# Pick products moved to GpSimd, ScalarE and TensorE, and the value gates loaded into two buffers of 8 tiles

## The reference

```
h = rms_norm(x);  q = h @ w_pq                        # 8 heads, two halves of 128
sc = q . sub_keys                                     # 2 x 128 scores per head
top 16 of each half -> 256 sums -> top 16 -> expert = i1 * 128 + i2;  gate = softmax(best)
a   = u_emb[expert] . h                               # one dot product per token, head, pick
out = sum over 8 * 16 picks of gelu(a) * gate * v_emb[expert]
```

## Time and profile before

| | us |
|---|---|
| median of three runs | 4348.66 |
| the profiled execution | 4346.32 |
| its span | 4344.6 |
| VectorE busy | 3200.2 (74%) |
| TensorE busy | 3476.6 (80%) |
| GpSimd busy | 1899.8 (44%) |
| ScalarE busy | 1453.4 (33%) |

### The profile page before, as it was taken

How to read it: one execution, slowest core, us unless ns; L and a number is a source line. 1 busy time by engine, 2 the same in 40 slices (tenths; PEclk the granted TensorE clock), 3 DMA queues, 4 the chain that set the end, 5 groups by cost and what they waited for, 6 DMA issues and landing times. The chain is left out here.

```text
span 4344.6 us, 46851 instructions
## 1 busy us (share of the span) xinstructions
PE 3476.6 (80%) x15298; PEld 2697.7 (62%) x15298; DVE 3200.2 (74%) x5528; ACT 1453.4 (33%) x2400; POOL 1899.8 (44%) x1508
## 2 busy tenths in 40 slices
PE   6999999997999987789899999733377777777775
PEld 5776667774778765577777777523355555555554
DVE  5677777777535137999999999899856666666667
ACT  3555555556524332232323232222211111111112
POOL 2443334433221314456565656455434444444443
PEclk9999999998999999899999999855588888888887
DMA  2111111102533225799999999898878888888785
GB/s 89 44 45 50 49 50 49 54 25 89 202 126 122 78 83 196 269 357 358 359 360 356 368 361 366 297 375 325 330 249 285 289 284 289 291 284 289 285 290 213
DMA packets 333363, 964.44 MB, mean 222 GB/s; under 512 B 30912, under 2 KB 96704, under 8 KB 330048
## 3 DMA queue, kind: packets, MB, share of 16 engines
q0 software_dynamic: 147456, 536.94, 33.3%
q1 hardware_dynamic: 183360, 390.95, 25.9%
q10 hardware_dynamic: 2304, 33.56, 1.9%
HBM read 861.18 MB, written 100.14 MB: 221 GB/s over the span
## 5 line engine op out<-in xcount | busy, mean ns | idle before, releaser
L2444 POOL DMA_INDIRECT spread_vrow<-in_v_rows,shared_pick_rows x512 | 712.4, 1391 | 769.7 <-DVE spread_y L2472 654.8
L1582 POOL DMA_INDIRECT ret_urow<-in_u_rows,shared_pick_rows x512 | 641.0, 1252 | 469.4 <-DVE ret_urow L2193 331.0
L157 PE MATMUL spread_banks<-spread_ahi,spread_vhi 128*128 128x512 f32 x1024 | 457.1, 446 | 344.7 <-DVE spread_alo L2484 260.8
L2472 DVE SCALAR_TENSOR_TENSOR spread_y<-spread_vrow,shared_pick_coef,spread_y 128x1024 f32<-128x1024 f32 x512 | 638.8, 1279 | 8.8 <-DMA spread_vrow<-in_v_rows,shared_pick_rows 8.8
L2193 DVE SCALAR_TENSOR_TENSOR ret_urow<-ret_urow,ret_h_rows 128x1024 f32<-128x1024 f32 x512 | 608.9, 1227 | 17.9 <-DMA ret_urow<-in_u_rows,shared_pick_rows 15.6
L157 PE MATMUL shared_carry<-ret_hhi,shared_w_hi 128*128 128x512 f32 x1152 | 474.2, 412 | 106.3 <-DVE shared_w_lo L1382 63.2
L157 PEld LDWEIGHTS spread_banks<-spread_ahi,spread_vhi 128*128 128x128 f32 x1024 | 213.6, 209 | 458.5 <-DVE spread_alo L2484 287.4
L157 PE MATMUL shared_carry<-shared_wide_hi,shared_w_hi 128*128 128x512 f32 x1152 | 458.3, 398 | 27.4 <-DVE shared_wide_lo L585 11.2
L158 PE MATMUL shared_carry<-ret_hlo,shared_w_hi 128*128 128x512 f32 x1152 | 464.9, 404 | 0.0
L159 PE MATMUL shared_carry<-shared_wide_hi,shared_w_lo 128*128 128x512 f32 x1152 | 453.7, 394 | 0.0
L158 PE MATMUL shared_carry<-shared_wide_lo,shared_w_hi 128*128 128x512 f32 x1152 | 453.7, 394 | 0.0
(11 more groups left out here) (295 smaller groups left out, 6921.2 us busy)
## 6 DMA issues: line engine op xcount, KB each, us to landing
spread_vraw<-in_peer_v SPq DMA_DIRECT2D x128, 512.0 KB, 6.9
shared_w_raw<-in_peer_u SPq DMA_DIRECT2D x65, 512.0 KB, 7.0
gelu_u<-shared_front SPq DMA_DIRECT2D x128, 256.0 KB, 8.0
gates<-spread_stage ACTq DMA_DIRECT2D x16, 2048.0 KB, 9.5
spread_act<-gelu_u SPq DMA_DIRECT2D x128, 256.0 KB, 5.3
spread_graw<-gates SPq DMA_DIRECT2D x32, 1024.0 KB, 15.5
ret_wraw<-in_peer_u SPq DMA_DIRECT2D x63, 512.0 KB, 6.8
shared_w_raw<-in_w_mix SPq DMA_DIRECT2D x56, 512.0 KB, 3.4
```

Of the source, the lines that this page charges most:

```text
L157: nc.tensor.matmul(out, whi, xhi, start=(first and i == 0), stop=False)
L1582: nc.gpsimd.indirect_dma_start(slots[s][:], None, u_rows, bass.IndirectOffsetOnAxis(tables.rows[:, t, hd * K + j:hd * K + j + 1], 0)).then ...
L2444: nc.gpsimd.indirect_dma_start(v_slots[s][:], None, v_rows, bass.IndirectOffsetOnAxis(tables.rows[:, t, j:j + 1], 0)).then_inc(row_loaded[ ...
L2472: nc.vector.scalar_tensor_tensor(out=y[:, t], in0=v_slots[s][:], scalar=tables.coef[:, t, j:j + 1], in1=y[:, t], op0=ALU.mult, op1=ALU.add ...
```

## The change

**Dot products.** From dot 34 on (the second block with dots) every fourth, 120 in all, is not done by VectorE. GpSimd multiplies the row in its slot by `h` (`product`), behind the fetches of the two next rows and after waiting for this row to land. ScalarE sums the products with a copy that accumulates (`sums`), behind the tile to whose place in the order the dot belongs (`due`). The slot is free when ScalarE has summed. The slots stay 7.

**Early rows of v.** In the one-hot stage TensorE weighs three of the four rows of each step: ScalarE scales the identity by the coefficients (`diag`, six buffers), TensorE multiplies it with the row (two plain f32 matmuls of 512 columns) and accumulates in four banks of PSUM, for tokens of blocks 0 and 1. VectorE adds these sums to `y` once, after the stage. The slots for rows of `v` go from 13 to 7, in the value groups too.

**Value gates.** `graw` becomes two buffers of 8 tiles (2 MB each, runs of 1 KB), loaded once per two groups. The activations' buffer moves to a place of its own, so that its first tiles are loaded before the last gates are stored.

```diff
@@ -1512,6 +1512,10 @@
+        FIRST_POOLED, POOL_BEHIND = dots_before(2), 2
+        pooled = [d >= FIRST_POOLED and d % 4 == 3 for d in range(DOTS)]
+        upto = {kind: [sum(p is kind for p in pooled[:d]) for d in range(DOTS + 1)] for kind in (True, False)}
...
@@ -1577,8 +1581,10 @@
                     pool.wait_ge(rows_made, hd + 1)
-                pool.wait_ge(dotted, d + 1)
-                pool.sem_inc(slot_held, 1)
+                if d >= ROWS_SLOTS:
+                    last = d - ROWS_SLOTS
+                    pool.wait_ge(pool_summed if pooled[last] else dotted, upto[pooled[last]][last + 1])
+                    pool.sem_inc(slot_held, 1)
...
@@ -1591,10 +1597,20 @@
             pool.wait_ge(x2t_stored, 16 * GT)
+            def product(d):
+                s, t = d % ROWS_SLOTS, d % (GT * K) % GT
+                pool.wait_ge(row_loaded[s], d // ROWS_SLOTS * 16 + 16)
+                nc.gpsimd.tensor_tensor(slots[s][:], slots[s][:], h_rows[:, t], ALU.mult).then_inc(pool_dotted, 1)
...
                 fetch(d)
+                if d >= POOL_BEHIND and pooled[d - POOL_BEHIND]:
+                    product(d - POOL_BEHIND)
...
                     give_low((d - ROWS_SLOTS + 1) // 3 + 3)
+            for d in range(DOTS - POOL_BEHIND, DOTS):
+                if pooled[d]:
+                    product(d)
...
@@ -1927,16 +1943,39 @@
+            summed_to = [0]
...
+            def sums(upto_dot):
...
+                for d in range(summed_to[0], max(upto_dot, summed_to[0])):
+                    if pooled[d]:
+                        hd, k, s = d // (GT * K), d % (GT * K), d % ROWS_SLOTS
+                        t, j = k % GT, k // GT
+                        act.wait_ge(pool_dotted, upto[True][d + 1])
+                        nc.scalar.activation(slots[s][:], slots[s][:], ACT.Copy,
+                                             accum_out=tables.coef[:, t, hd * K + j:hd * K + j + 1]).then_inc(pool_summed, 1)
+                summed_to[0] = max(upto_dot, summed_to[0])
...
+            def due(tile):
...
+                n = tiles.place[tile]
+                b = max(b for b in range(FIRST_DENSE, BLOCKS) if STARTS[b] <= n)
+                first, after = dots_before(b), dots_before(b + 1)
+                return min(after, first + (after - first) * (n - STARTS[b]) // (STARTS[b + 1] - STARTS[b]))
...
                     expert(e)
+                    sums(due(("expert", 1, e)))
...
                             query(b + 1, c)
+                            sums(due(("query", b + 1, c)))
...
                         copy_scores(b + 1)
+            sums(DOTS)
...
@@ -1946,7 +1985,8 @@
                 parts_high(r)
-            act.wait_ge(dotted, DOTS + ROWS_SLOTS)
+            act.wait_ge(dotted, upto[False][DOTS])
+            act.wait_ge(pool_summed, upto[True][DOTS])
...
@@ -2187,6 +2227,8 @@
                 for d in range(d0, d1):
+                    if pooled[d]:
+                        continue
...
@@ -2320,7 +2362,8 @@
         QC = NC // NQ
-        SV = 13
+        SV = 7
+        G8 = 2 * E
...
@@ -2331,8 +2374,8 @@
-        act = m.at("act", [P, E, TD], F32, at(36))
-        graw = m.at("graw", [P, QUARTERS, E, W], F32, at(44))
+        act = m.at("act", [P, E, TD], F32, at(176))
+        graw = [m.at(f"graw{i}", [P, QUARTERS, G8, W], F32, at(x)) for i, x in enumerate((36, 160))]
...
@@ -2342,19 +2385,23 @@
+        DIAGS = 6
+        diag = [m.at(f"diag{i}", [P, P], F32, at(184) + 512 * i) for i in range(4)] + [m.at(f"diag{4 + i}", [P, P], F32, at(189) + 512 * i) for i in range(2)]
...
+        y_sums = banks[:, NB:NB + 4].rearrange("p (t h) n -> p t (h n)", h=2)
...
@@ -2365,12 +2412,27 @@
         FIRST_PICKS = EARLY * N
+        BY_PE = 3
+        order, made_of = [], [0] * GT
+        for d in range(PICKS):
+            if d < FIRST_PICKS:
+                n, i = divmod(d, EARLY)
+                t = (BY_PE * n + i) % 2 if i < BY_PE else 2 + n % 2
+            else:
+                t = min((t for t in range(GT) if t != order[-1][0]), key=lambda t: made_of[t])
+            order.append((t, made_of[t]))
+            made_of[t] += 1
+        by_pe = [d < FIRST_PICKS and d % EARLY < BY_PE for d in range(PICKS)]
+        upto = {kind: [sum(p is kind for p in by_pe[:d]) for d in range(PICKS + 1)] for kind in (True, False)}
+        PE_PICKS = upto[True][PICKS]
+        before = [max([x for x in range(d) if order[x][0] == order[d][0] and by_pe[x] is by_pe[d]], default=None) for d in range(PICKS)]
...
@@ -2384,11 +2446,11 @@
-            def load_gates(g):
-                if g:
-                    sync.wait_ge(weighted, E * g)
-                sync.dma_start(graw[:].rearrange("p n e t -> p n (e t)"),
-                               g_out[:, :, E * g:E * g + E, :].rearrange("n p j t -> p n (j t)")).then_inc(g_loaded, 16)
+            def load_gates(i):
+                if i >= 2:
+                    sync.wait_ge(weighted, G8 * (i - 1))
+                sync.dma_start(graw[i % 2][:].rearrange("p n e t -> p n (e t)"),
+                               g_out[:, :, G8 * i:G8 * i + G8, :].rearrange("n p j t -> p n (j t)")).then_inc(g_loaded[i % 2], 16)
...
@@ -2401,14 +2463,14 @@
                 load_values(1, q)
+            for e in range(E):
+                load_tile(0, e)
...
                 sync.wait_ge(stored[s], 16 * (QUARTERS // SLOTS))
-            for e in range(E):
-                load_tile(0, e)
             load_gates(0)
+            load_gates(1)
...
                 load_tile(1, e)
-            load_gates(1)
...
@@ -2418,7 +2480,8 @@
                 load_tile(g, 3)
-                load_gates(g)
+                if g % 2 and g < NG - 1:
+                    load_gates(g // 2 + 1)
...
@@ -2437,10 +2500,16 @@
             def fetch(d):
-                s, t, j = d % SV, d % GT, d // GT
-                pool.wait_ge(picked, d + GT + 1)
-                pool.sem_inc(slot_held, 1)
+                s, (t, j) = d % SV, order[d]
+                if d >= SV:
+                    last = d - SV
+                    pool.wait_ge(weighed if by_pe[last] else picked, upto[by_pe[last]][last + 1])
+                    pool.sem_inc(slot_held, 1)
...
@@ -2466,18 +2535,24 @@
                 for d in range(d0, d1):
-                    s, t, j = d % SV, d % GT, d // GT
+                    if by_pe[d]:
+                        continue
+                    s, (t, j) = d % SV, order[d]
                     dve.wait_ge(row_loaded[s], d // SV * 16 + 16)
-                    dve.wait_ge(picked, d + SV + 1)
+                    if before[d] is not None:
+                        dve.wait_ge(picked, upto[False][before[d] + 1])
+                    elif t < 2:
+                        dve.wait_ge(y_joined, t + 1)
...
                 dve.wait_ge(a_loaded[e], g * 16 + 16)
-                if e == 0:
-                    dve.wait_ge(g_loaded, g * 16 + 16)
+                gates, i = graw[g // 2 % 2], g % 2 * E + e
+                if i == 0:
+                    dve.wait_ge(g_loaded[g // 2 % 2], g // 4 * 16 + 16)
                 tokens = act[:, e].rearrange("p (n t) -> p n t", t=W)
-                tt(tokens, tokens, graw[:, :, e], ALU.mult).then_inc(weighted, 1)
+                tt(tokens, tokens, gates[:, :, i], ALU.mult).then_inc(weighted, 1)
...
@@ -2508,6 +2583,9 @@
                 split(0, e)
+            dve.wait_ge(weighed, PE_PICKS)
+            for t in range(2):
+                tt(y[:, t], y[:, t], y_sums[:, t], ALU.add).then_inc(y_joined, 1)
...
@@ -2578,10 +2656,21 @@
                     mm.then_inc(g_done, 1)
+                for d in range(EARLY * n, EARLY * n + BY_PE):
+                    s, (t, j) = d % SV, order[d]
+                    last = d + 2 >= FIRST_PICKS - EARLY + BY_PE
+                    pe.wait_ge(row_loaded[s], d // SV * 16 + 16)
+                    pe.wait_ge(diag_made, upto[True][d + 1])
+                    for h in range(2):
+                        mm = nc.tensor.matmul(y_sums[:, t, h * H:h * H + H], diag[upto[True][d] % DIAGS][:], v_slots[s][:, h * H:h * H + H],
+                                              start=(j == 0), stop=last)
+                    mm.then_inc(weighed, 1)
...
                     q, dp = k // QC, slice(k % QC * P, k % QC * P + P)
+                    if g == 0 and k in (4, 6):
+                        pe.wait_ge(y_joined, k // 2 - 1)
...
@@ -2615,6 +2704,13 @@
                     values(0, n)
+                for d in range(EARLY * n, EARLY * n + BY_PE):
+                    x, (t, j) = upto[True][d], order[d]
+                    if x == 0:
+                        act_eng.wait_ge(ident_made, 1)
+                    if x >= DIAGS:
+                        act_eng.wait_ge(weighed, x - DIAGS + 1)
+                    nc.scalar.activation(diag[x % DIAGS][:], ident[:], ACT.Copy, scale=tables.coef[:, t, j:j + 1]).then_inc(diag_made, 1)
...
@@ -2641,7 +2737,7 @@
             for t in range(GT):
-                act_eng.wait_ge(picked, SV + 1 + PICKS + t)
```

(22 more changed lines are left out.)

## The result

The kernel after the change takes 4474.07 us (median of 4 runs, 4468.40 to 4487.82) beside 4348.22 for the kernel before on the same chip: ratio 1.0296, 95% interval 1.0267 to 1.0324. I had forecast 4308. The profiled execution has a span of 4472.1 us, 127.5 longer than before.

What follows compares the result with a forecast made beforehand. VectorE and DMA were taken to bound the retrieval, VectorE the one-hot stage, a wait for gates the value groups. From 4346.3 us, -220 - 5 - 15 + 200 = -40 gave 4306, 4308 on the runs' scale; range 4090 to 4490.

Steps and rivals of the forecast that it cites:

- 10.1 us for four, +200 us: Retrieval: GpSimd's landing, product and fetches make four dots take 10.1 us against 8.44, +200 us over 120 moved dots.
- ScalarE's sums hide and free their slots as now: Retrieval: ScalarE's 120 sums, about 1.06 us each, hide in its idle time and free slots as before.
- exclusion of VectorE and GpSimd: Retrieval: operations with two SBUF inputs exclude each other, so VectorE's four dots take 9.1 us, +82 us.
- rival B: Retrieval: GpSimd's wait for landing eats all the gain at a landing of 6.2 us; at 7.2, 4463 us; chance 0.27.
- the forecast ring: Retrieval, GpSimd's cycle: landing 5.9, product 2.45, gap 0.2, next fetch 1.25, gap 0.3: 10.1 us for four dots.
- L: Retrieval: time from a row's fetch to its landing, taken as 5.9 us; earlier medians 8.0, and 6.2 in a less crowded stretch.
- Rival A: Retrieval: exclusion costs little, four dots stay at DMA's pace of 8.44 us, total 4108 down to 4079; chance 0.20.
- GpSimd's own 8.9: Retrieval: without a wait, GpSimd's four fetches and one product take 8.9 us for four dots, +55 us.
- Two resources are full at once: Retrieval before the change: VectorE busy 954 of 977 us and DMA share 0.97 at 360 GB/s, both full.
- 29.4: Value groups: gates' wait goes, DMA bounds a group at 29.4 us against 36.5, -220 us; bounds -344 and -124.
- Case D's 32.5 us: Value groups: gates' wait goes but 7 slots or DMA hold a group at 32.5 us, total 4404; chance 0.08.
- One-hot stage: One-hot stage: DMA last, step from 9.57 to 9.1 us, -15 us; bounds -25 and +164; f32 product 0.93 to 1.85 us.

Runs made afterwards that it cites:

- the first experiment: Changed kernel with all 512 dot products back on VectorE; TensorE's early rows and the two gate buffers stay: 4045.96 us, ratio 0.930 to the kernel before.
- fifth: Changed kernel with GpSimd's product four fetches behind, slots free at that product, ScalarE's 120 sums left out: 4162.99 us, ratio 0.958 to the kernel before.
- seventh: Changed kernel, product still two fetches behind, slots free at GpSimd's product, ScalarE's 120 sums left out: 4369.99 us, ratio 1.005 to the kernel before.
- second: Changed kernel with GpSimd's product four fetches behind its row in place of two, nothing else: 4407.27 us, ratio 1.013 to the kernel before.
- eighth experiment: Changed kernel without dots on GpSimd, VectorE multiplying only 128 of 1024 columns in each of the 512 dots: 3953.06 us.
- tenth run: The kernel before with slots for rows of v cut from 13 to 7, nothing else: 4348.57 us, ratio 1.0007.
- fourth experiment: Changed kernel with all dots and early rows on VectorE; only two gate buffers and 7 slots left: 4038.43 us, ratio 0.929 to the kernel before.
- eleventh experiment: Changed kernel without dots on GpSimd, TensorE weighing its rows before a step's short matmuls: 4017.27 us, ratio 0.924 to the kernel before.

## Why the prediction was wrong

**The step that failed** is the retrieval, "10.1 us for four, +200 us", with the sentence that ScalarE's sums hide and free their slots as now. It measured +428 by the first experiment, and the stretch +420 where more than 300 was to refute the forecast. The runs split this into three, one taken away at a time:

| | from | us |
|---|---|---|
| exclusion of VectorE and GpSimd, with GpSimd's own time | fifth - first | +117 |
| GpSimd standing before a row that has not landed | seventh - fifth | +207 |
| slots held until ScalarE has summed | after - seventh | +104 |

Each part depends on the order in which the others are taken away: ScalarE's round costs 244 us with the product four behind (second - fifth) and 104 with two, because the first ring hides part of it. Against the forecast's +200 the first two parts are 324, so the ring was sized 124 us too small, and the sums, put at nothing, add 104. The value groups' 84 us gave part of this back.

**The wait for landing.** The mechanism was right, and named as rival B, but the forecast ring was 1.2 us too short: 10.1 against 11.26 in the seventh. Its parts there: from fetch d to the start of its product 6.6 us in the mean, where I took 5.9; the product 2.6 where I took 2.45; and the fetch behind a product 1.62 in the mean (mostly 1.78), where I took the mean over all fetches, 1.25. With 0.15 and 0.3 of gaps that is 11.3. I had chosen 5.9, below the median that I had in the earlier trace rows, on the argument that the queue would be empty; L was 6.3 in the median, and rival B's point of decision was 6.2. The sum is so steep there (120 us per us of L) that the choice decided the sign: with 6.3 it gives 4356.

**ScalarE's sums** were costed by its busy time, 287 of 977 us. Most of its idle time is spent waiting for TensorE (888 of 1402 us after the change), and a sum's place in the order is behind such a wait (second experiment). TensorE in turn waits for VectorE's low parts, 414 us in 91 times where it was 98 in 41 in the stretch of the earlier trace rows. So VectorE's wait for a late row comes back as a later sum and a later slot; how much of the cost runs through this longer ring no run shows. "The slots they free are those of dots seven back" gave the wrong comfort: with seven slots the sum has the time of four fetches when the product stands two behind, and of two when it stands four behind, where one came 15.6 us after the product.

**The exclusion** held: +82 forecast, +117 measured with GpSimd's own time in it. I took 79% of a product as lost to VectorE. By its busy share in the fifth, four dots take 9.05 us of VectorE's time (0.957 of 9.45) and took 8.24 before (0.976 of 8.44): 0.8 more though one of them, 1.22, was moved, so about 2.0 of a product's 2.46 us are lost, 82%. The other 0.2 of the 1.0 us is VectorE idle. Rival A, the exclusion costing little, is refuted. Its "GpSimd's own 8.9" was right too, and would have cost +55 alone by my sum; a run with GpSimd's time but no exclusion is missing.
The Trainium skill (GPSIMD Engine Reference, Key points) has the two engines contend for their SBUF interfaces; the fifth run agrees, with dots of 1611 ns beside products of 2458.

**DMA's ceiling.** "Two resources are full at once" was wrong: at 360 GB/s DMA was following VectorE (eighth experiment: 383 GB/s, 93 us less). This error ran through the value groups too. The wait went as forecast, but a group is 26.1 us by the count above, not 29.4: -304 in place of -220, inside its bounds. Case D's 32.5 us is refuted by the same count, with seven slots in place; the tenth run adds that they cost nothing in the kernel before.
The Trainium skill (DMA: Bandwidth & Descriptors, Where 436 GB/s comes from) puts HBM's limit for one core near 358 GB/s, which is a stack's 716 divided by its two cores. This kernel runs on one core, and its traces do not agree with 358 as a limit: 391 GB/s over 750 us after the change, 395 in the fourth experiment.

**One-hot stage.** Forecast 9.57 to 9.1 us; measured (3560.41 - 3255.43)/31 = 9.84, +8 us and not -15, inside the bounds. Relief of VectorE came (148 of 240 us busy), the granted clock rose from 0.58 to 0.90, and the step gained nothing, since the rows' slots stood behind TensorE's wait for the same step's gates, as the eleventh experiment shows. The waits from 3300 to 3540:

```profile
POOL spread_vrow L2513 <- PE spread_banks L2665: 116.2, 56, 10.0
DVE spread_y L2546 <- DMA spread_vrow<-in_v_rows,shared_pick_rows: 99.1, 15, 10.3
```

With that order mended (eleventh experiment) the step is 8.90 and DMA 363 GB/s at 0.96. So DMA as the stage's new bound fits only then. The f32 products were 592 ns a record, so 1.18 for each, between my 0.93 and 1.85.

**What held:** the dots' mean above 1217 ns (1407), products of 2.3 to 3.5 us behind waits of 1 to 3 us and more, the wait for gates gone from all groups but the first (22.0 us there, 20.1 before). The granted clock in the retrieval fell from 0.95 to 0.84, with TensorE busy in 70% of it and not 90%. DMA's share fell to 0.74, below the 0.83 forecast. Rival B's 4463 lies 11 us from the result, but it had the same mechanism at L = 7.2, and so stood in for ScalarE's part too; that closeness is in part luck.

## What to carry to other kernels

An operation given to the engine that issues the gathers costs its duration and, unless it stands far enough behind its fetch (four fetches here), also part of the landing time of the row that it waits for, since everything behind it in that queue is issued late: write the ring out (landing, operation, next issues, with the duration that an issue has just there) and see which constant decides the sign before choosing a value for it. Here an idle engine would have hidden the added operation only if its place in that engine's order had been reached in time; where the operation also frees a buffer, add its delay to the ring. A DMA share of 0.97 beside an engine at 98% did not say which of the two bounds: shorten the engine's work once and look at the rate.

## What was not expected of the hardware

DMA moved 391 to 395 GB/s in the value groups, and 383 beside gathers in the eighth experiment, where no slice of 109 us of the kernel before passed 375. Runs of 1 KB in place of 512 B in a tenth of that traffic, with half as many loads of it, raised it from 382 to 395. An indirect fetch issued right behind a product on GpSimd takes mostly 1.78 us (51 of 79 in the seventh experiment), and 0.94 in the median when it follows another fetch.
